# Queries' RMS norm applied as a scale of the exponential, and the rotary swap done by transfers, in a one-core decoder layer

## What is computed

```python
def rms_norm(x, g):
    y = xf * lax.rsqrt(jnp.mean(xf * xf, axis=-1, keepdims=True) + EPS)
    return (y * g.astype(jnp.float32)).astype(x.dtype)

def rope(x, pos):                       # half = 32
    x1, x2 = xf[..., :half], xf[..., half:]
    return jnp.concatenate([x1 * cos - x2 * sin, x2 * cos + x1 * sin], axis=-1)

"qa": rope(rms_norm(qa.reshape(b, t, H_A, HEAD_DIM), q_norm_a), pos),
"ka": rope(rms_norm(ka.reshape(b, t, HKV_A, HEAD_DIM), k_norm_a), pos),
"qi": rope(qi.reshape(b, t, H_IDX, D_IDX), pos),
"qb": rope(rms_norm(qb.reshape(b, t, H_B, HEAD_DIM), q_norm_b), pos),
"kb": rope(rms_norm(kb.reshape(b, t, HKV_B, HEAD_DIM), k_norm_b), pos),

logits = einsum('qngd,qknd->qngk', qg, ks) * (HEAD_DIM ** -0.5)
p = softmax(where(valid, logits, -inf))
```

## Time and profile before

| | |
|---|---|
| median of 3 runs | 649.51 us (649.44 to 654.71) |
| the profiled execution, its own time | 652.55 us |
| its span, first to last instruction | 650.5 us |
| PE busy | 641.0 us (99%) |
| DVE busy | 424.4 us (65%) |
| ACT busy | 299.4 us (46%) |
| POOL busy | 154.9 us (24%) |
| mean granted clock of TensorE | 0.995 |

### The profile page before, as it was taken

The page is one execution under the profiler, slowest core; times in us unless marked ns, Lnnn a source line. Parts: engine busy times, 40 slices in busy tenths (PEclk is TensorE's granted clock), DMA queues, the critical chain, the costliest instruction groups (busy, mean ns, idle before and its releaser), DMA issues.

```text
span 650.5 us, 12966 instructions
## 1 busy us (share of the span) xinstructions
PE 641.0 (99%) x4804; PEld 617.9 (95%) x4804; DVE 424.4 (65%) x657; ACT 299.4 (46%) x489; POOL 154.9 (24%) x217
## 2 busy tenths in 40 slices
PE   8999999999999999989999999999999999999998
PEld 6999999999999999866989989999999999999998
DVE  5766666665455587999896846977656566665441
ACT  7634353443334434545543557545444434353330
POOL 1477774000011237347511300161000000000000
PEclk9999999999999999999997999999999999999999
DMA  8777666455455454423231232554354555546530
GB/s 335 266 227 221 218 219 223 142 171 177 159 173 193 135 182 138 129 65 98 98 102 63 96 124 91 173 196 151 118 185 154 169 161 162 167 145 207 170 112 19
DMA packets 32121, 103.04 MB, mean 158 GB/s; under 512 B 5136, under 2 KB 5840, under 8 KB 32080
## 3 DMA queue, kind: packets, MB, share of 16 engines
q1 hardware_dynamic: 27648, 96.22, 44.8%
q0 software_dynamic: 3616, 4.73, 2.7%
q10 hardware_dynamic: 816, 1.54, 0.6%
HBM read 100.77 MB, written 1.70 MB: 158 GB/s over the span
## 4 chain that ended last, share of the span: by engine, by line
PE 88%; DVE 6%; issue 2%; ACT 2%; DMA 1%; POOL 1%; SPq 0%; ACTq 0%; POOLq 0%
PE ps L1104 28%; PE ps L1106 27%; PE ps L1105 27%; DVE wlo L796 2%; DVE roots L1023 1%; DVE acc L961 1%; PE ps L1309 1%; DMA x<-in_x 1%; PE ps L1232 1%; PE ps L1264 1%; PE ps L1295 1%; PE ps L1347 1%; ACT whi L556 1%; PE ps L1128 0%; DVE tmp L1017 0%
## 5 line engine op out<-in xcount | busy, mean ns | idle before, releaser
L796 DVE TENSOR_TENSOR wlo<-raw,whi 128x1024 fp32r<-128x1024 f32 (+1 forms) x181 | 227.6, 1261 | 122.1 <-ACT whi L556 121.9
L1104 PE MATMUL ps<-nhi,whi 128*128 128x288 f32 x952 | 287.7, 302 | 0.1
L1105 PE MATMUL ps<-nlo,whi 128*128 128x288 f32 x952 | 282.0, 296 | 0.0
L1106 PE MATMUL ps<-nhi,wlo 128*128 128x288 f32 x952 | 281.1, 295 | 0.0
L556 ACT ACTIVATE whi<-raw 128x1024 fp32r<-128x1024 f32 (+1 forms) x181 | 182.4, 1030 | 137.6 <-PE ps L1106 130.2
L1104 PEld LDWEIGHTS ps<-nhi,whi 128*128 128x128 f32 x952 | 179.2, 188 | 4.6 <-issue 3.5
L1105 PEld LDWEIGHTS ps<-nlo,whi 128*128 128x128 f32 x952 | 179.5, 189 | 0.7
L1106 PEld LDWEIGHTS ps<-nhi,wlo 128*128 128x128 f32 x952 | 180.0, 189 | 0.0
L1104 PE MATMUL ps<-hhi,whi 128*128 128x288 f32 x336 | 99.5, 296 | 0.0
L1105 PE MATMUL ps<-hlo,whi 128*128 128x288 f32 x336 | 99.1, 295 | 0.0
L1106 PE MATMUL ps<-hhi,wlo 128*128 128x288 f32 x336 | 98.8, 294 | 0.0
(11 more groups left out here) (182 smaller groups left out, 704.6 us busy)
## 6 DMA issues: line engine op xcount, KB each, us to landing
raw<-in_weights SPq DMA_DIRECT2D x165, 512.0 KB, 3.4
raw<-in_weights SPq DMA_DIRECT2D x16, 384.0 KB, 3.6
raw<-in_weights SPq DMA_DIRECT2D x4, 256.0 KB, 4.3
kt<-in_cache_kidx_a POOLq DMA_DIRECT2D x32, 32.0 KB, 3.0
kt<-in_cache_k_b POOLq DMA_DIRECT2D x16, 64.0 KB, 2.8
kt<-in_cache_k_a POOLq DMA_DIRECT2D x32, 32.0 KB, 2.9
vb_pg<-in_cache_v_b POOLq DMA_DIRECT2D x16, 64.0 KB, 3.3
cst<-in_constants ACTq DMA_DIRECT2D x1, 980.0 KB, 8.0
```

Source lines behind the costliest of these rows:

```text
L796: nc.vector.tensor_tensor(wlo[:, v % NU, 0:nk, 0:w], raw[:, v % NR, 0:nk, 0:w], whi[:, v % NU, 0:nk, 0:w].bitcast(F32), ALU.subtract).then ...
L1104: nc.tensor.matmul(out[0:w, 0:N], h, hi, start=start and i == 0, stop=False)
L1105: nc.tensor.matmul(out[0:w, 0:N], h, lo, start=False, stop=False)
L1106: ins = nc.tensor.matmul(out[0:w, 0:N], l, hi, start=False, stop=stop and done is not False and i == len(ks) - 1)
```

## The change

**Norm of queries.** `NORMED` keeps only the two keys. The eight query units still get their squares and gains on ACT, but the squares now go to PE as the stationary operand, in three fp32 matmuls of 8 columns a unit (tokens 0 to 127, 256 to 287, 128 to 255), against a selector with 8 columns. So the sums of squares stand with tokens on rows and heads on columns, in bank 5 for `qb` and bank 4 for `qa`. DVE adds the epsilon (slots 14 and 18), POOL raises to the power -0.5 (slots 15 and 19, after the rotation and the copies to `qz`), PE spreads the sample tokens' scales to the sample layout (slots 16 and 20, two fp32 matmuls of 8 columns), and DVE reduces them to columns (slots 17 and 21). Each exponential takes the scale as its per-row factor, and each maximum is multiplied by it first (one more small DVE instruction per softmax step).

**Norm of keys.** The rotation now comes first and the product with the reciprocal root after it.

**Rotation.** The swap is made by SP: four transfers of 32 partitions x 288, from the unit to `rot_tmp`, after the load of the unit eleven ahead. DVE's sine product reads `rot_tmp` in place of the bank. The buffer is free when the rotation two before is final (`z_final`), and SP waits for that.

**Other.** The buffer `roots` moves; the exponential's table is loaded after the keys' last root (slot 7) and no longer in slot 17; the exponentials of slot 17 come before ACT's split there.

```diff
-NORMED = [U_KA, U_KB] + list(range(U_QB, U_QA + 4))
+NORMED = [U_KA, U_KB]
+SCALED = NORMED + list(range(U_QB, U_QA + 4))
+POWER_SLOT, EXPAND_SLOT = {15: MOBA, 19: DSA}, {16: MOBA, 20: DSA}
+            def swap_halves(u):
+
+                i = index_among(u, ROTATED)
+                if u in SCALED:
+                    sp.wait_ge(zg_ready, index_among(u, SCALED) + 1)
+                else:
+                    sp.wait_ge(z_ready, u + 1)
+                if i >= 2:
+                    sp.wait_ge(z_final, i - 1)
+                for b in range(P // HALF_HD):
+                    to = (b ^ 1) * HALF_HD
+                    sp.dma_start(rot_tmp[to:to + HALF_HD, i % 2, :],
+                                 zloc[u][b * HALF_HD:(b + 1) * HALF_HD]).then_inc(swapped[i % 2], 16)
...
                     for v in range(first["P"], first["G2"]):
                         load(v)
+                        if v - first["P"] - SWAP_AFTER in ROTATED:
+                            swap_halves(v - first["P"] - SWAP_AFTER)
...
-                    pool.wait_ge(swapped, i + 1)
+                    pool.wait_ge(swapped[i % 2], SWAP_INC * (i // 2 + 1))
                     nc.gpsimd.tensor_tensor(z, z, c_(C_COS, N), ALU.mult).then_inc(rot_cos, 1)
                     pool.wait_ge(rot_cos, i + 1)
                     pool.wait_ge(rot_ready, i + 1)
-                    nc.gpsimd.tensor_tensor(z, z, rot_tmp[:, i % 2, :], ALU.add).then_inc(z_final, 1)
+                    nc.gpsimd.tensor_tensor(z, z, rot_tmp[:, i % 2, :], ALU.add).then_inc(rot_sum if normed_u else z_final, 1)
+                    if normed_u:
+                        n = index_among(u - ROT_DELAY, NORMED)
+                        pool.wait_ge(rot_sum, n + 1)
+                        pool.wait_ge(zrstd_ready, n + 1)
+                        nc.gpsimd.tensor_tensor(z, z, roots[:, n % N_ROOTS, :], ALU.mult).then_inc(z_final, 1)
...
-                if u - 1 in NORMED:
-                    i = index_among(u - 1, NORMED)
-                    pool.wait_ge(zg_ready, i + 1)
-                    pool.wait_ge(zrstd_ready, i + 1)
-                    nc.gpsimd.tensor_tensor(zloc[u - 1], zloc[u - 1], roots[:, i % 2, :], ALU.mult).then_inc(zn_ready, 1)
+                if u in POWER_SLOT:
+                    k = POWER_SLOT[u] - 1
+                    pool.wait_ge(qms_ready, k + 1)
+                    if k == 0:
+                        pool.wait_ge(minus_half, 1)
+                    for r, c0, c1 in ((P, 0, 2 * HEADS), (NS_TOK, 2 * HEADS, 3 * HEADS)):
+                        nc.gpsimd.tensor_tensor(rq[0:r, k, c0:c1], qms[0:r, k, c0:c1],
+                                                eps_col[0:r, 3:4].to_broadcast([r, c1 - c0]), ALU.pow).then_inc(rq_ready, 1)
...
                         ins = nc.scalar.activation(probs[:, m % 2, h * w:(h + 1) * w], ps[m % 2][:, h * w:(h + 1) * w],
-                                                   ACT.Exp, bias=nmax[:, 4 * m + h:4 * m + h + 1],
+                                                   ACT.Exp, bias=nmax[:, 4 * m + h:4 * m + h + 1], scale=q_scales(m)[:, h:h + 1],
...
                     nc.vector.tensor_reduce(nmax[:, 4 * m:4 * m + nh], ps[m % 2][:, 0:nh * w].rearrange("p (h k) -> p h k", h=nh),
-                                            AX, ALU.max, negate=True).then_inc(max_done, 1)
+                                            AX, ALU.max, negate=True).then_inc(max_raw, 1)
+                    dve.wait_ge(max_raw, m - 7)
+                    if m == 8 or m == 16:
+                        dve.wait_ge(rq_ready, 2 * kind)
+                    nc.vector.tensor_tensor(nmax[:, 4 * m:4 * m + nh], nmax[:, 4 * m:4 * m + nh], q_scales(m), ALU.mult)\
+                        .then_inc(max_done, 1)
...
-                    dve.wait_ge(swapped, i + 1)
-                    if i >= 2:
-                        dve.wait_ge(z_final, i - 1)
-                    nc.vector.tensor_tensor(rot_tmp[:, i % 2, :], ps[4][:, 0:N], c_(C_SIN, N), ALU.mult).then_inc(rot_ready, 1)
+                    dve.wait_ge(swapped[i % 2], SWAP_INC * (i // 2 + 1))
+                    nc.vector.tensor_tensor(rot_tmp[:, i % 2, :], rot_tmp[:, i % 2, :], c_(C_SIN, N), ALU.mult).then_inc(rot_ready, 1)
...
+                if u - 1 in SCALED[len(NORMED):]:
+                    i = index_among(u - 1, SCALED)
+                    k, j = divmod(i - len(NORMED), 4)
+                    bank = ps[Q_BANK[k + 1]]
+                    pe.wait_ge(zsq_ready, i + 1)
...
+                    for t in (0, 2, 1):
+                        r = P if t < 2 else NS_TOK
+                        ins = nc.tensor.matmul(bank[0:r, t * HEADS:(t + 1) * HEADS], act_tmp[:, i % 2, 0, t * P:t * P + r],
+                                               c_(C_QSEL + (4 * k + j) * HEADS, HEADS), start=j == 0 and t == 0, stop=j == 3 and t == 1)
+                    ins.then_inc(zms_done, 1)
+                if u in EXPAND_SLOT:
+                    k = EXPAND_SLOT[u] - 1
+                    pe.wait_ge(rq_ready, 2 * k + 2)
+                    for g in range(2):
+                        ins = nc.tensor.matmul(ps[Q_BANK[k + 1]][:, (4 + g) * HEADS:(5 + g) * HEADS],
+                                               c_(C_EXP + g * P, P, NS_TOK), rq[0:NS_TOK, k, 2 * HEADS:3 * HEADS],
+                                               start=True, stop=True)
+                    ins.then_inc(rq_ps, 1)
...
-                if u - ROT_DELAY in ROTATED:
-                    i = index_among(u - ROT_DELAY, ROTATED)
-                    pe.wait_ge(z_ready, u - ROT_DELAY + 1)
-                    if u - ROT_DELAY in NORMED:
-                        pe.wait_ge(zn_ready, index_among(u - ROT_DELAY, NORMED) + 1)
-                    if i:
-                        pe.wait_ge(rot_ready, i)
-                    nc.tensor.matmul(ps[4][:, 0:N], c_(C_SWAP, P), zloc[u - ROT_DELAY], start=True, stop=True).then_inc(swapped, 1)
```

More of the change, by code:

```diff
@@ L62, with head_of @@
 C_HSEL = C_EXPT + 2 * NS_TOK
-C_ALL = C_HSEL + HEADS
+C_QSEL = C_HSEL + HEADS
+C_ALL = C_QSEL + 2 * 4 * HEADS
+IDX, MOBA, DSA = 0, 1, 2
+def head_of(kind, block, half):
+    return block + 4 * half if kind == MOBA else 2 * block + half
 def shape_constants():
@@ L75, in shape_constants @@
     p = np.arange(P)
-    c[p ^ half, C_SWAP + p] = 1.0
     c[p, C_ID + p] = 1.0
@@ L90, in shape_constants @@
     c[:, C_HSEL:C_HSEL + HEADS] = rh[:, None] == np.arange(HEADS)[None, :]
+    for kind in (MOBA, DSA):
+        for m in range(4):
+            for half in range(2):
+                c[half * HD:(half + 1) * HD, C_QSEL + ((kind - 1) * 4 + m) * HEADS + head_of(kind, m, half)] = 1.0 / HD
     return c
@@ L257, in build @@
         kv, _ = sb("kv", [P, 5, N], at=blk(36))
[L258 removed]
+        roots, _ = sb("roots", [P, N_ROOTS, N], at=blk(16))
         masksb, _ = sb("masksb", [NS_TOK, NK_S], BF16, at=blk(43))
@@ L296, in build @@
         rinv = new("rinv", [P, 4 * N_STEPS])
+        qms = new("qms", [P, 2, 3 * HEADS])
+        rq = new("rq", [P, 2, 3 * HEADS])
+        rsel = new("rsel", [P, 2, HEADS])
+        rcol = new("rcol", [P, 2, 2])
         wi_p = new("wi_p", [P, 2, HEADS])
@@ L390, in last_of_bank, with q_scales @@
             return u - 2 if u >= 6 else u - 4
+        Q_BANK = {MOBA: 5, DSA: 4}
+        def q_scales(m):
+            kind, form, i = step_kind(m)
+            if form == 2:
+                return rcol[:, kind - 1, i:i + 1]
+            half, blocks, _ = step_heads(form, i)
+            c0 = form * HEADS + head_of(kind, blocks[0], half)
+            step = head_of(kind, 1, 0) - head_of(kind, 0, 0)
+            return rq[:, kind - 1, c0:c0 + step * (len(blocks) - 1) + 1:step]
         def out_views(t, bank, kind, form):
@@ L514, in _ @@
             for u in range(U_END):
-                if u - 1 != NORMED[-1]:
-                    for m in STEPS_OF_SLOT.get(u, []):
-                        if 8 <= m:
-                            weigh(m)
+                for m in STEPS_OF_SLOT.get(u, []):
+                    if 8 <= m:
+                        weigh(m)
                 if u - ROT_DELAY in ROTATED:
@@ L708, in _ @@
                 for m in STEPS_OF_SLOT.get(u, []):
-                    if not last_root:
-                        attend(m)
+                    attend(m)
                 if u == TOK_SLOT:
@@ L979, in outputs_lo @@
                     dve.wait_ge(out_hi, g + 1)
+                    if g == 3:
+                        dve.wait_ge(z_final, len(ROTATED))
                     lo_t, hi_t = (blo, bhi) if kind == MOBA else (alo, ahi)
@@ L991, in _ @@
                         search_step(c)
-                late = [m for m in STEPS_OF_SLOT.get(u, []) if m < 8 or u - 1 == NORMED[-1]]
+                late = [m for m in STEPS_OF_SLOT.get(u, []) if m < 8]
                 for m in STEPS_OF_SLOT.get(u, []):
@@ L1022, in _ @@
                     dve.wait_ge(zroot_ready, i + 1)
-                    nc.vector.reciprocal(roots[:, i % 2, :], roots[:, i % 2, :]).then_inc(zrstd_ready, 1)
```

(20 more changed lines are left out.)

44 lines of the change are left out of this document (23 added, 21 removed).

## The result

The changed kernel takes 664.52 us (median of four runs, 660.51 to 664.85); the kernel before, run beside it, 650.26 (649.44 to 654.71). The ratio is 1.017, 95% interval 1.0144 to 1.0196: slower by 1.7%, where I forecast 643.5 us and gave "slower by over 1%" a chance of 0.12. The profiled execution has a span of 663.2 us, 12.7 more than before.

The account below looks back on a forecast made before the run. PE, busy 641.0 of 650.5 us, was taken to bound the kernel. Work saved, 5.1 us, plus gaps, 0.9, made 6.0: from 649.5 to 643.5 us. Range 640.3 to 649.3, leaving out C.

Parts of the forecast that it names:

- The power itself is in no row ... I take 0.4: POOL's two power instructions: 0.4 us a pair, between 0.2 and 1.6, bounded by POOL's copies and sums.
- rival C: Slots 16 and 20: power slow on GpSimd, each us of a pair costing twice; 656.7 us at 7 a pair; chance 0.12.
- the wait: PE waiting for `rq` from POOL before the spreading: 2.2 us in slot 16 and 0.4 in slot 20.
- PE's waits that come with the transfers: SP's swap transfers, slots 3 to 9: just keep up, cost 0; issue 0.45 us each, landing 1.7.
- Rival B: Slot 16: TensorE's clock falls because PE does little for some 4 us; price 3.4 us, giving 646.9; chance 0.12.
- PE's work: PE's matmuls: loses 11.0 us, gains 4.8 for sums of squares and 1.1 for spreading, so falls by 5.1.
- the sums of squares: Three short fp32 matmuls a query unit on PE: 0.60 us a unit, 4.8 for eight, bounds 0.48 and 0.81.
- The gap at slot 15: PE's wait before slot 15's indexer logits: stays, 1.3 us after the change against 1.43 before.
- Slot 18's and slot 4's gaps: PE's waits for POOL's weighing (0.70 and 0.34 us) and for `rot_ready` before the swap (0.34): all gone.
- A: Slots 12 to 18: DVE was the true limit, so all gaps close and `rq`'s wait is hidden; 640.3 us, chance 0.17.
- The median: Kernel before: its 649.5 us median read as runs without the half-clock stretch, and used as the sum's starting point.

Follow-up runs that it names:

- The subtraction: Changed kernel with GpSimd's powers replaced by subtractions of the same shapes in the same place: 653.67 us, ratio 1.0009 to the kernel before.
- the filling matmuls: Changed kernel with unread matmuls (56 and 44) issued on PE before its waits for the powers in slots 16 and 20: 659.13 us, ratio 1.01.
- the norm alone: Changed kernel with powers in slots 14 and 18 before the rotation, but the swap back on PE's matmul: 649.5 us, ratio 0.9953 to the kernel before.
- early powers: Changed kernel with both powers a slot earlier on GpSimd (14 and 18), ahead of the rotation: 645.37 us, ratio 0.9901; repeated 647.41, ratio 0.992.
- the third buffer: Changed kernel with powers a slot earlier before the rotation, outputs issued by SP, and three `rot_tmp` buffers: 644.43 us, ratio 0.9864; repeated 643.28, 0.9843.

## Why the prediction was wrong, and where it was right

**The step that failed: "The power itself is in no row ... I take 0.4".** Measured 4.54 and 4.50 us a pair. My upper bound, 1.6, came from the wrong class of rows: products and sums, which POOL runs over 128 partitions at 36,864 numbers in 0.8 us. A copy and a sum bound other copies and sums; they say nothing on a power, and I wrote as much under rival C ("no row shows a power") without letting it widen the bound. C's own count was off as well: it has 384 elements, and the pair has 2,304. The range left C out. The subtraction in the same place is the proof that it is this term: it took the ratio from 1.017 to 1.0009, some 10.5 us. With C's own rule (each us of a pair counted twice) the surplus of 4.1 gives 8.2 us; the wait grew from the forecast 2.6 to 12.7, by 10.1.

**The power is not the whole miss.** With the subtraction the kernel is what I had priced, a cheap pair at slots 15 and 19, and it took 653.67 us, level with the kernel before, where the sum gives 646.6 from that kernel's typical time of 652.6 (see the median, below). Three terms make up most of these 7.1 us. The wait for `rq` is 4.1 us for the 2.6 forecast. PE's waits that come with the transfers, which I put at 0, are 1.6 us in that profile. And the clock falls in the wait, a term that I kept out of the sum: the seven slower of the ten runs lie some 3.5 us above the other three.

**The rest of that wait is the place.** With the power made cheap PE still waits 2.6 and 1.5 us. For slot 16 my count, 2.2, was nearly right, though it took the copies at 0.63 us and they took 1.52 there. For slot 20 I took 0.4 "between no wait and 1 us"; it was 1.1 more.

**Rival B came too, with C and without it.** I gave the fall of the clock in slot 16 a price of 3.4 and a chance of its own. But a long wait for the power is just what makes PE stand still, so C brings B with it, and twice (slots 16 and 20): 5.6 us by the windows, about 5 by the filling matmuls. Nor does B need C: with the subtraction, behind waits of 2.6 and 1.5 us, the clock fell too, so it belonged in the sum at least in part. My case C at 7 us a pair ended at 656.7; the pair was only 4.5, and the time was 664.5. The chances of C and B should have been tied together, and C's break-even of 3.4 us a pair was too high for that reason: it counted the wait alone.

**PE's work: right in sum.** Forecast -5.1, measured -4.9 (busy time less the half that half speed costs); no swap is left on PE, and 23 long matmuls are gone. In detail the sums of squares are dearer than I took: from start to start 0.78 us (267.06 to 267.84) and 0.69 (261.46 to 262.15) a unit, where I had 0.60. The Trainium skill, page "TensorE: Matmul & The Clock Gate", section "LDWEIGHTS (loading the stationary operand)", gives by its rule of stationary columns over 1.2 the 0.48 of the prediction, an estimate. The trace lies above it by more than I allowed:

```profile
267.06 0.76 PE L1415 MATMUL ps<-cst,act_tmp 128*128 128x8 f32 x6
267.84 0.70 PE L1306 MATMUL ps<-kv,qi 64*128 64x256 f32 x4
```

**The indexer's slots: half right.** The gap at slot 15 stayed, as I said, since the chain goes through ACT's high half: 0.87 there and 1.29 before slot 14's logits, 2.2 for the 1.3 forecast. Without the reciprocal the low half waits for ACT (1.11 us at 275.16), so the chain kept its length and PE, arriving sooner, waits for it. Slot 18's and slot 4's gaps went, as forecast. A was wrong for this change: the gaps did not all close. They nearly did where the swap stays on PE: with the norm alone and early powers PE waits 0.34 us in slot 4 and 0.56 us once more in the whole mixer, where it has 0.48 us more to do in each slot.

**The transfers: costs too low, cover nearly enough.** One transfer's issue takes 0.58 us in place of 0.45 (four take 2.41), and it lands in 2.1 in place of 1.7, SP's timeline and the line by itself:

```profile
242.93 2.41 SPq L483 DMA_DIRECT2D tmp<-qi  x4
```

```profile
DMA to landing us min/median/max: 1.8/2.1/3.1
```

Against my zero, PE lost 0.70 and 0.74 us (L1431 and L1178 in the list of waits); the version with the norm alone has neither wait, and the third buffer closed the second. I also missed that DVE's sine product, which read one operand from PSUM, now reads both from SBUF and meets POOL's cosine product.

**The median: wrong.** I read 649.51 as runs without the fall of the clock. In four more sets of runs the kernel before has medians of 652.59, 652.76, 652.85 and 652.57, and the typical one of these 67 runs takes 652.5 to 652.8 at a granted clock of 0.994 or 0.995; of the four at 1.000 three took 649.5 to 649.7 and one 650.5. So runs without the fall do take what I read, but they are rare, and the three shown at first were not typical. Against the typical time the sum of -6.0 is 646.6. The early powers came to 645.4 and 647.4, near that, but in part by luck: they have no wait for `rq` at all, where the sum had 2.6 us, and this makes up for the gaps and transfers that it had too low. The kernel that the sum describes is the one with the subtraction, and there it missed by 7 us.

## What to carry to other kernels

An operation that no row shows is bounded by rows of its own class or not at all; a cheap add on an engine does not bound its power, and if the step from which it turns the result round lies within reach, its chance belongs in the forecast. A slow instruction costs nothing where its engine idles: moving the same 4.5 us by a slot and ahead of the rotation turned +1.7% into -1.0% and, repeated, -0.8%. And a wait of TensorE is priced with the clock that falls in it, and parts of a change are judged together where one may make the room that the other needs: the transfers gave nothing alone and 2 to 5 us beside the norm.
